# Stick-breaking and window attention scores with stacked high and low halves: two full-array matmuls per head, the swapped queries made by DMA

## What is computed

```
u    = rmsnorm(h, g);  sb_q, sb_k, sb_v, sb_g, sw_q, sw_k, sw_v, sw_g = split(u @ w_in)
# stick-breaking, blocks of 128 queries, all keys up to the block's end
z    = (sb_q * scale) @ sb_k.T;  log_beta = log_sigmoid(z);  log_1m = where(causal, log_beta - z, 0)
a    = where(causal, exp(log_beta + reversed_exclusive_cumsum(log_1m)), 0);  sb_o = (a @ sb_v) * silu(sb_g)
# window: chunks of 64 queries against their own and the previous chunk and the 16 meta keys
s    = (rope(sw_q) * scale) @ rope(sw_k).T;  p = softmax(concat(s, sink))[:-1];  sw_o = (p @ sw_v) * silu(sw_g)
h    = h + concat(sb_o, sw_o) @ w_out;   output = rmsnorm(h)[16:]
```

## Time and profile before

| | before |
|---|---|
| median of 3 runs | 1206.63 us (1204.77 to 1209.02) |
| the profiled execution's own time | 1204.28 us |
| its span, first to last instruction | 1202.5 us |
| TensorE matmul, busy | 1169.5 us (97%) |
| TensorE weight loads, busy | 1069.6 us (89%) |
| VectorE, ScalarE, busy | 688.1 us (57%), 435.7 us (36%) |
| granted TensorE clock, mean | 0.999 of full speed |

### The profile page before, as it was taken

The page is one execution under the profiler, slowest core; times in us unless marked ns, Lnnn a source line. Parts: engine busy times, 40 slices in busy tenths (PEclk is TensorE's granted clock), DMA queues, the critical chain, the costliest instruction groups (busy, mean ns, idle before and its releaser), DMA issues.

```text
span 1202.5 us, 22513 instructions
## 1 busy us (share of the span) xinstructions
PE 1169.5 (97%) x8922; PEld 1069.6 (89%) x8922; DVE 688.1 (57%) x1370; ACT 435.7 (36%) x1189; POOL 2.6 (0%) x5
## 2 busy tenths in 40 slices
PE   7999999999999999999999999999999999999998
PEld 6988888988888989889999888888888898888998
DVE  6645454456457567754583554645444956866533
ACT  7323333333344345521231432333334434453113
POOL 0000000000000000000000000000000000000000
PEclk9999999999999999999999999999999999999999
DMA  5611010101021121141322010101011212104203
GB/s 200 235 36 36 19 36 19 36 19 35 19 55 48 23 58 51 42 173 35 143 73 69 19 36 19 36 19 36 19 36 27 65 35 49 53 7 171 70 8 141
DMA packets 102839, 69.31 MB, mean 58 GB/s; under 512 B 37952, under 2 KB 95296, under 8 KB 102736
## 3 DMA queue, kind: packets, MB, share of 16 engines
q1 hardware_dynamic: 101872, 66.55, 18.5%
q10 hardware_dynamic: 864, 1.32, 0.3%
HBM read 49.82 MB, written 12.71 MB: 52 GB/s over the span
## 4 chain that ended last, share of the span: by engine, by line
PE 89%; DVE 6%; ACT 2%; issue 2%; DMA 0%; SPq 0%; ACTq 0%; DVEq 0%
PE psum L869 41%; PE psum L857 20%; PE psum L921 7%; PE psum L933 6%; PE psum L950 6%; PE psum L982 2%; PE psum L1047 1%; DVE mix L1388 1%; PE psum L1019 1%; PE psum L994 1%; PE psum L1012 1%; DVE UL L1398 1%; PE psum L963 1%; ACT P_late L1275 1%; PE psum L892 1%
## 5 line engine op out<-in xcount | busy, mean ns | idle before, releaser
L869 PE MATMUL psum<-UH,WH 128*128 128x384 f32 (+2 forms) x1632 | 536.0, 328 | 7.6 <-DVE UL L1398 4.5
L869 PE MATMUL psum<-UL,WH 128*128 128x384 f32 (+2 forms) x1632 | 522.6, 320 | 0.0
L857 PE MATMUL psum<-UH,WL 128*128 128x384 f32 (+2 forms) x1632 | 517.1, 320 | 1.3 <-DVE WL L1441 1.3
L869 PEld LDWEIGHTS psum<-UH,WH 128*128 128x128 f32 x1632 | 306.6, 188 | 17.1 <-DVE UL L1398 5.7
L857 PEld LDWEIGHTS psum<-UH,WL 128*128 128x128 f32 x1632 | 307.2, 188 | 2.0 <-DVE WL L1441 1.9
L869 PEld LDWEIGHTS psum<-UL,WH 128*128 128x128 f32 x1632 | 307.3, 188 | 0.0
L1261 ACT ACTIVATE PT<-psum 128x512 f32<-128x512 f32 (+5 forms) x260 | 116.7, 492 | 19.7 <-PE psum L933 18.3
L1252 ACT ACTIVATE X<-psum 128x264 f32<-128x264 f32 (+9 forms) x240 | 91.1, 431 | 78.3 <-PE psum L921 77.8
L1521 DVE TENSOR_TENSOR_SCAN X<-X,stick 16x16 f32<-16x16 f32 (+5 forms) x144 | 100.4, 737 | 23.2 <-ACT X L1252 22.9
L933 PE MATMUL psum<-ident,X 128*128 128x128 f32 x576 | 91.0, 283 | 3.7 <-ACT Vn L1215 2.7
L1524 DVE TENSOR_TENSOR_SCAN X<-X 128x352 f32<-128x352 f32 (+4 forms) x96 | 86.3, 939 | 7.7 <-ACT X L1252 7.7
(11 more groups left out here) (171 smaller groups left out, 1000.5 us busy)
## 6 DMA issues: line engine op xcount, KB each, us to landing
w_raw<-in_w_in SPq DMA_DIRECT2D x36, 512.0 KB, 3.9
h_spill<-X SPq DMA_DIRECT2D x16, 520.0 KB, 6.4
X<-h_spill SPq DMA_DIRECT2D x16, 520.0 KB, 5.4
w_raw<-in_w_in SPq DMA_DIRECT2D x32, 256.0 KB, 3.8
w_raw<-in_w_out SPq DMA_DIRECT2D x16, 256.0 KB, 3.0
w_raw<-in_w_out SPq DMA_DIRECT2D x32, 128.0 KB, 3.3
vT<-dvT SPq DMA_DIRECT2D x40, 50.0 KB, 2.0
vT<-dvT SPq DMA_DIRECT2D x40, 48.0 KB, 2.0
```

The source lines that it names most:

```text
L857: return pe.matmul(out_columns, WL[:, j % 2, k, :], UH[:, k, uses], start=False, stop=(k == KT - 1))
L869: pe.matmul(out_columns, WH[:, j % 2, k, :], u[:, k, uses], start=(k == 0 and u is UH), stop=False)
```

## The change

The two operands are stacked over the array's rows. For head 0 the key's high part stands in rows 0..63 and its low part in rows 64..127 (for head 1 the other way round), and the queries likewise. One full-array matmul then gives high x high plus low x low, and a second one, with the query's halves swapped, gives the two mixed terms. So per head and piece there are two matmuls over 128 rows where there were three over 64. The low x low term is now in the sum.

- ACT's and DVE's split of q, k and of rope's output becomes two instructions, one per half of 64 partitions; DVE reads one half and writes the other.
- The swapped queries are made by SP's DMAs: `q_swap` per block, in a ring of two, each pair of DMAs of 64 KB issued when the Z two blocks back is done; `q_window` per window unit, one buffer in the place of `q_swap`, issued when the unit before has its scores; `q_meta` for the meta units.
- TensorE waits for the swap: in a Z step ahead of head 0's second matmul, in SZ ahead of everything.
- SZ 0 and SD 0 move behind the first gate projection, SZ 1 behind the second.
- `PT` has four slots instead of five, `ones` 16 columns instead of 128 (16 were used).

```diff
-Z_RING, T_RING, PT_RING, O_RING = 2, 2, 5, 2
+Z_RING, T_RING, PT_RING, O_RING = 2, 2, 4, 2
+Q_RING = 2
...
+        if p == 0:
+            q[0] += [("q_swap", 0, b) for b in range(Q_RING)]
...
+        for b in range(BLOCKS):
+            later = divmod(p * BLOCKS + b + Q_RING, BLOCKS)
+            if later[0] < PAIRS:
+                scores[b].append(("q_swap",) + later)
...
-        out = [("SZ", 0), ("SD", 0)] + fill[0] + [("SZ", 1)] + fill[1]
+        out = fill[0] + [("SZ", 0), ("SD", 0)] + fill[1] + [("SZ", 1)]
...
+    for n, (hp, r) in enumerate(UNITS):
+        if r == META_UNIT:
+            behind = ("SZ", n - 9) if hp else ("Z", PAIRS - 1, BLOCKS - 1, len(key_segments(BLOCKS - 1)) - 1)
+        else:
+            past = [m for m in range(n) if UNITS[m][1] != META_UNIT]
+            behind = ("SZ", past[-1]) if past else ("Z", PAIRS - 1, BLOCKS - 1, len(key_segments(BLOCKS - 1)) - 1)
+        at = 1 + max(steps.index(behind), steps.index(("rope_low", 2 + 2 * hp, unit_chunk(r))))
+        steps.insert(at, ("window_swap", n))
...
+                def swap_queries(p, b):
+                    g, slot = p * BLOCKS + b, (p * BLOCKS + b) % Q_RING
+                    sp.wait_ge(q_in.sem, q_in.at(l, 3 * p + chunk_of(q_start(b) + n_queries(b) - 1) + 1))
+                    if g >= Q_RING:
+                        gone = divmod(g - Q_RING, BLOCKS)
+                        sp.wait_ge(z_full.sem, z_full.at(l, 2 * scans_until(*gone)))
+                    queries = slice(q_start(b), q_start(b) + n_queries(b))
+                    for a in (0, 64):
+                        other = 64 - a
+                        sp.dma_start(q_swap[a:a + 64, slot, :, 0:n_queries(b)].bitcast(F32),
+                                     stick_qk[p % 2][other:other + 64, 0:2, queries].bitcast(F32))\
+                            .then_inc(q_swapped[slot].sem, 16)
...
+                def swap_window(n_unit):
+                    (hp, r), rows = UNITS[n_unit], 2 * META
+                    sp.wait_ge(rope_low_made.sem, rope_low_made.at(l, ROPE_AT[2 + 2 * hp, unit_chunk(r)]))
...
+                    else:
+                        before = max(n for n in range(n_unit) if UNITS[n][1] != META_UNIT)
+                        sp.wait_ge(z_full.sem, z_full.at(l, Z_AT["SZ", before] + 2))
+                    for a in (0, 64):
...
+                        sp.dma_start(to.bitcast(F32), source.bitcast(F32)).then_inc(landed_at.sem, 16)
...
-                    for i, (q, k) in enumerate(((0, 2), (0, 3), (1, 2))):
-                        for h in range(2):
-                            if i == 0 and use + h >= Z_RING:
-                                pe.wait_ge(z_read.sem, z_read.at(l, use + h - Z_RING + 1))
-                            rows = slice(64 * h, 64 * h + 64)
-                            ins = pe.matmul(z_bank[0:n_queries(b), h, 0:hi - lo], QK[rows, q, queries],
-                                            QK[rows, k, lo:hi], start=(i == 0), stop=(i == 2))
-                            if i == 2:
-                                ins.then_inc(z_full.sem, 1)
+                    for h in range(2):
+                        if use + h >= Z_RING:
+                            pe.wait_ge(z_read.sem, z_read.at(l, use + h - Z_RING + 1))
+                        z, keys = z_bank[0:n_queries(b), h, 0:hi - lo], QK[:, 2 + h, lo:hi]
+                        pe.matmul(z, QK[:, h, queries], keys, start=True, stop=False)
+                        if i == h == 0:
+                            pe.wait_ge(q_swapped[g % Q_RING].sem, q_swapped[g % Q_RING].at(l, 32 * swaps_of(g % Q_RING, g + 1)))
+                        pe.matmul(z, swapped[:, h, :], keys, start=False, stop=True).then_inc(z_full.sem, 1)
...
+                        pe.wait_ge(window_swapped.sem, window_swapped.at(l, 32 * (swaps_until(n_unit) + 1)))
...
+                            pe.matmul(z, SQ[:, 2 * hp + g, a:a + rows_out], keys, start=True, stop=False)
+                            ins = pe.matmul(z, swapped, keys, start=False, stop=True)
...
-                        act.activation(stick_qk[p % 2][:, 0, chunk_uses(c)], src, ACT.Copy).then_inc(qh_made.sem, 1)
+                        QK = stick_qk[p % 2][:, 0:2, chunk_uses(c)]
+                        act.activation(QK[0:64, 0], src[0:64], ACT.Copy)
+                        act.activation(QK[64:128, 1], src[64:128], ACT.Copy).then_inc(qh_made.sem, 1)
...
-                        dve.tensor_tensor(QK[:, high + 1, chunk_uses(c)], src, QK[:, high, chunk_uses(c)].bitcast(F32),
-                                          ALU.subtract).then_inc(done.sem, 1)
+                        dve.tensor_tensor(QK[64:128, 0], src[0:64], QK[0:64, 0].bitcast(F32), ALU.subtract)
+                        dve.tensor_tensor(QK[0:64, 1], src[64:128], QK[64:128, 1].bitcast(F32), ALU.subtract)\
+                            .then_inc(done.sem, 1)
...
-                    for (source, to), (_, high) in zip(roped(c, e, 1), roped(c, e, 0)):
-                        ins = dve.tensor_tensor(to, source, high.bitcast(F32), ALU.subtract)
+                    for g in range(2):
+                        for source, high, to in roped(c, e, g):
+                            ins = dve.tensor_tensor(to, source, high.bitcast(F32), ALU.subtract)
```

## The result

The changed kernel takes 1245.53 us (median; 1239.38 to 1246.61) where the kernel before takes 1207.08: ratio 1.0309, interval 1.0270 to 1.0348, about 37 us slower. The forecast was 11 us slower, with 1226 as the top of the range. The profiled execution took 1246.61.

What follows compares the result with a forecast made beforehand. TensorE's own work was taken as the bound (89% of the span); -13.3 stick scores, +6.0 window scores, +1.4 halves and +17.0 window swaps made +11.1, giving 1217.7 us, range 1201 to 1226.

Steps and rivals of the forecast that it cites:

- stick scores with q's and k's halves: Stick stage: cheaper full-array passes and shorter bank waits, -13.3 us; half copies uncovered at each layer's first Z, +1.4.
- window passes: Window scores: thirty units at +0.2 us each for eight full passes and the shape change into SAV, +6.0.
- rope's halves on ScalarE and VectorE: Rope's split into two 64-partition instructions: hidden, no term of its own in the sum.
- SZ 0 behind a projection, without its swap: Window start: SZ 0 moved behind a projection (24 x 0.182 = 4.4 us); no cost for the move itself.
- waits for the window's swaps: TensorE stalls per layer: SZ 9 3.9 us, SZ 6 1.9, SZ 0 2.2, smaller ones 0.5; two layers +17.0.
- clock behind SZ 0 and SZ 9: Lower clock after the window's swap stalls: not in the sum, only a rival with +3 to +7 us.
- a rival of its own: Clock falls in the stalls: up to 1.7 us each, two to four falls, 1221 to 1225 us; chance 0.25.
- smaller ones, 0.5 a layer: Window swap stalls at SZ 5, 8, 17 and the block above: 0.5 us a layer.
- It hides because: Doubled half instructions, some 25 us on either engine: hidden, since a bank's next user is a whole projection (4.2 us) away.
- At the first Z the term: Each layer's first Z: half instructions uncovered, some 0.35 us on each engine, +1.4 for two layers.
- the two array terms: Stick stage: passes and shape changes -8.5 us, shorter bank waits -4.8 over eight pairs; together -13.3.
- the relief of the banks: Three stick steps a pair wait less for their scores' bank, 0.2 us saved of about 0.43 each; -4.8.

Runs made afterwards that it cites:

- run 1: Stacked stick scores alone, with q's and k's halves, their swaps and the ring of four; window attention as in the kernel before: 1199.54 us, ratio 0.9944.
- run 7: Kernel without window swaps, SZ 0 in its old place, plus rope's copies over 128 rows as in the kernel before: 1204.46 us, ratio 0.9988.
- run 6: Changed kernel without window swaps or their waits, SZ 0 back ahead of the first fill projection: 1208.38 us, ratio 1.0020.
- run 5: Changed kernel without window swaps or their waits; the second matmul of each window score takes unswapped queries: 1213.70 us, ratio 1.0060.
- run 3: Changed kernel with unread full-array matmuls ahead of the swap waits at SZ 0 (11) and SZ 9 (24): 1232.64 us, ratio 1.0217.
- run 4: Kernel with only the stick scores stacked, plus the swaps of units 10 and 9 and TensorE's wait at SZ 9: 1211.48 us, ratio 1.0044.
- run 11: Stacked stick scores alone, halves signalled apart, turned values copied ahead of q's halves for the third and fourth pair only: 1196.91 us, ratio 0.9924.
- run 10: Stacked stick scores alone; ScalarE signals after each half copy, VectorE starts after the first: 1198.29 us, ratio 0.9932.
- run 8: Changed kernel with the swaps of units 0 and 9 queued ahead of the meta swaps of units 1 and 10: 1238.12 us, ratio 1.0257.
- run 12: Stacked stick scores alone with both repairs, plus eight unread matmuls ahead of each layer's first Z: 1198.00 us, ratio 0.9933.

## Why the prediction was wrong

What failed is the sum: it put the clock, rope's halves and SZ 0's new place at nothing, where the runs show 19.8 us, and the gain of the stick scores at nearly twice its size. Its steps beside what the runs price them at (differences of the ratios; each is good to 2 to 4 us, the clock's to 5):

| step | predicted | measured | by |
|---|---|---|---|
| stick scores with q's and k's halves | -13.3 + 1.4 = -11.9 | -6.8 | run 1 |
| window passes | +6.0 | +5.3 | run 7 less run 1 |
| rope's halves on ScalarE and VectorE | 0 | +3.9 | run 6 less run 7 |
| SZ 0 behind a projection, without its swap | 0 | +4.8 | run 5 less run 6 |
| waits for the window's swaps | +17.0 | +18.9 | run 3 less run 5 |
| clock behind SZ 0 and SZ 9 | 0 in the sum | +11.1 | the change less run 3 |
| sum | +11.1 | +37.2 | |

**The clock** was the largest miss. The prediction had it as a rival of its own ("two to four falls give +3 to +7", 0.25), when runs 3 and 4 show that it comes with the predicted waits: whoever forecasts waits of 2 to 4 us in a stream that, past its start, never stood so long has to add it to the likeliest case. It was also too small, for it took "half clock over 3.4 us" for one wait. Behind SZ 9 it lasted 10.2, and some waits of 1.25 to 2.7 us (SZ 6, SZ 17, the first Z, SZ 0) were followed by a stretch too: eight falls more than before. The price of one, "up to 1.7", was right: 1.6 in run 4. By that price the 41 us more at the lower level are worth some 19 us (an estimate); the 11.1 of the table is the part behind SZ 0 and SZ 9, the rest stands in the other rows.

**The swaps' waits** were well placed, and their sum came out near in part by luck. SZ 9 waited 4.5 (3.9 predicted), SZ 0 2.2 and 2.7 (2.2). SZ 6 was overrated (0.3 and 1.25 against 1.9), and the "smaller ones, 0.5 a layer" were SZ 5, SZ 8 and SZ 17 with 3.8 us a layer. What was too much at SZ 6 and too little at these stood against each other. The 18.9 holds some clock as well, for run 3 still fell to the lower level behind SZ 17.

**SZ 0's place.** The prediction read the move only for the swap that it gives time to. It left out that SZ 0 itself gives cover to SZ 1, the exponentials and unit 0's transposes, and that all of these now stand a projection closer to their inputs: waits of 0.5 and 1.24 and a stretch at the lower clock, once a layer.

**Halves.** "It hides because ... all later ones leave a bank's next user a whole projection away" looked only at the bank's next user. The instructions did cost as much again (0.52 for 64 rows as for 128), but they also stand ahead of other work on a queue that runs in order: q's second half ahead of the copy of turned values (+2.2 in four waits), k's ahead of block 8's sigmoids (below), rope's ahead of the low halves that SZ 0 needs (its waits are 2.0 in run 6, 0.5 in run 7) and of the copies of transposed weights (1.3, and none in run 7). At the first Z the term was right: 1.84 against 1.02, so +1.6 against +1.4.

**Array.** Passes, ways in and ways out went as the prediction says, stick and window, but for the 0.10 behind transposes, which is a bank wait. By the lag of the projections the stick stage between the first Z and the window gained 4.1 us a layer in run 1, with 1.1 us of new waits for turned values in it: 5.2, where the two array terms give 6.65. The step where the rest is missing is block 8's second one. TensorE's and ScalarE's timelines there, and ScalarE's before:

```profile
210.85 0.60 PE L1013 MATMUL psum<-ident,X 128*128 128x128 f32 x4
211.73 0.44 PE L1001 MATMUL psum<-qk_odd 128*128 128x352 f32 x1 [0.28 <-ACT X L1340]
212.01 0.32 PE L1004 MATMUL psum<-qk_odd,q_swap 128*128 128x352 f32 x1
...
212.50 0.34 PE L949 MATMUL psum<-UH,WH 128*128 128x400 f32 x1
```

```profile
210.44 0.38 ACT L1256 ACTIVATE qk_even<-psum 64x256 fp32r<-64x256 f32 x1 [3.33 <-PE psum L937]
210.82 0.38 ACT L1257 ACTIVATE qk_even<-psum 64x256 fp32r<-64x256 f32 x1
211.23 0.79 ACT L1340 ACTIVATE X<-psum 128x336 f32<-128x336 f32 x2
```

```profile
209.74 0.79 ACT L1252 ACTIVATE X<-psum 128x336 f32<-128x336 f32 x2 [0.35 <-PE psum L921]
```

With its transposes the step takes 1.65 (210.85 to 212.50), before 1.70: the sigmoid that frees its bank stands behind k's second half copy, where it used to wait for TensorE. In the last pair, where no such copy stands there, it takes 1.25, and block 5's second step mostly gained what was forecast (0.44 against 0.40). So the relief of the banks was sized rightly, and of the missing 5 us 2.4 (0.4 in three pairs of two layers) and 2.2 are half copies ahead of other work on ScalarE; the rest is block 2's swap and 3.4 us at the lower clock at the first Z. No run moved k's half copies, so the 2.4 are read from the timelines alone. The Trainium skill, "TensorE: Matmul & The Clock Gate", Part 3, has weight loads overlap only across row groups; by that rule the new full matmuls would each show a load, and the trace denies it for the new stick ones as it did for the projections (0.205 to 0.21 for 456 columns, 0.46 ns each column). The Trainium skill, "TensorEngine Tiling (Array Packing)", Key Properties, says that changing the tiling mode drains TensorE; the trace agrees, with 0.10 in the first pass behind AV_rest and no such step behind a projection.

**Left open.** Whether a second buffer for the window's swapped queries, or another queue, would cover the swaps was not tried: without any swap, and with SZ 0 in its old place, the window part still loses 9 us (run 6 less run 1), so a cover of the swaps alone does not make it pay. Why equal waits are followed by stretches of different length, or by one here and by none there, is not settled: 1.84 us at the first Z by one in the changed kernel's first layer and by none in its second, 1.45 us there by one in run 11's profile and by none in run 10's, 1.50 at SZ 8 by none, 1.34 at SZ 17 by one.

## What to carry to other kernels

Cost a new wait on a saturated TensorE at its length plus, as a likely case, a stretch at the lower clock (here 1.6 us for each 3.4 us of it, up to 10 us long); if the wait can't be removed, unread matmuls in it may pay, but look first whether what follows only waits for the same transfer. A change of several parts should be split before it is judged: here the stick part won 6.8 us, 9.2 with two repairs, under a window part that lost 43. And when an instruction is doubled, the cover to look for is that of everything behind it on its engine, not only of its own reader.

## What the runs showed of the hardware that was not expected

The granted clock fell after some waits of 1.25 to 2.7 us too, though not after all of them (1.84 us at the second layer's first Z, 1.50 at SZ 8), and after one wait of 4.5 us TensorE ran 8 us fully busy at 1.2 GHz before the level came back (468.5 to about 476.5 in the stretches above). With twenty-four matmuls that nobody reads, 4.3 us of work in a wait of 5.1, it stayed at 2.4 GHz. At the lower level TensorE arrived later at its next wait, so a wait and a slow stretch hid each other: in run 8 a wait shrank from 4.5 to 1.07 us without its end moving, 2.2 us of it by TensorE's lateness, and in run 12 a slow stretch that was removed came back as a wait. An instruction over 64 rows took as long as one over 128 of the same columns, on VectorE (0.52 us in the mean of both) and on ScalarE (0.50 us for 400 columns).
